# Order of the output products inside a block of a gated-linear-attention, pooling and memory-attention layer on Trainium2

## The chip, the cores and the metric

The kernel runs on one core of one Trainium2 chip. The metric is device time in microseconds (us). The kernel before took 1407.87 us as the median of 3 runs (1406.61 to 1410.97).

## The reference

One decoder layer over `x` of 4096 rows by 1024, with a memory of 256 rows. Three mixers read one input projection, and one output projection adds them back:

```python
h = rmsnorm(x, norm_g)
q_g,k_g,v_g,gk_lr,gate_g,u_p,gate_p,q_m,gate_m = split(h @ w_in)
gk    = log_sigmoid(gk_lr @ w_gk_up + b_gk) / 16          # per-step log decay
o_gla = rmsnorm(gla_chunked(q_g, k_g, v_g, gk)) * silu(gate_g)   # 4 heads, chunks of 64, state carried along
o_pool= (multiscale_pool(u_p) @ pool_w) * pool_scale * silu(gate_p)
o_mem = softmax(q_m k_m^T / 8) v_m * silu(gate_m)         # k_m, v_m from rmsnorm(mem)
y     = rmsnorm(x + concat(o_gla, o_pool, o_mem) @ w_out, final_g)
```

In `gla_chunked` the state of a chunk is the decayed state of the chunk before plus `k_end^T v`; a head's output is its masked scores times `v` plus `q` times the state.

## The kernel before

The sequence is cut into 16 blocks (steps 0 to 15) of 256 rows, each with four chunks of 64. All large products are made of f16 high and low parts, three matmuls for each product. The engines each have their own instruction list and meet at semaphores; the order on each engine is the order in which its code is written. No scheduler changes it. Steps 0 to 3 multiply whole weight blocks (`whole`); steps 4 to 15 use a seven-product form (`phase`, `product`), for which ACT and POOL also make sums and differences of the normalised input.

A step `i` on TensorE (PE) is, in order:

- the low-rank product (L758), the first queries and keys product, then the decay logits (L777), which wait for ACT's copy `lrs` of the low-rank result. That copy (L1183) waits in ACT's queue, and also for `mix_g`, the end of the head products of step `i - 1` on VectorE (DVE), because `lrs` lies in the memory of `osq[1]`;
- all other input products, then the values (`values`, L662 on `wv`);
- transposes, scores and memory scores, and between and behind them the output projection of block `i - 1`, cut into four quarters of 24 matmuls of 128x512 (`quarter(n)`, `out_proj`, L662 on `ring`). Quarters 0 and 2 write PSUM bank 0, quarters 1 and 3 bank 1. Each quarter's result is added on DVE to the residual (`add_rows`, L1633, called `rows(n)`), and a quarter that uses a bank again waits for that addition;
- `states(0)`, `states(1)` (L900): the four chunk products from which DVE builds the carried state, `state(0)` to `state(3)` (L1884, two instructions each);
- `head_out(0, 5)`, `head_out(1, 4)` (L909, L915): the heads' products, the first behind `s_ok` of `state(2)`, the second behind that of `state(3)`;
- the product with the memory's values (L970), which waits for the DMA transposes (`d_turn`) of the softmax weights; it signals `pe_pv`;
- `head_ms(0)`, `head_ms(1)` (L923): sums of squares of the heads, which wait for ACT's squares (L1421).

On DVE the order at that place is `p_low(2)`, `p_low(3)` (L1868, the low parts of the softmax weights, behind ACT's L1377), `rows(1)`, `state(2)`, `state(3)`, `norm_rows`, `rows(2)`, the pool's and the memory's gated products, `rows(3)`, and the two heads (`head`, L1893 and L1895). On ACT, behind the squares of the heads, stand two copies of the input's sums (`x_mixed`, L1067) that wait for `pe_pv`, the Ln and Exp of the heads' norms (L1433, L1436), two more `x_mixed` copies, of which the last waits for a POOL subtraction (L2062) at the end of a chain that the first copy starts, and then `lrs` (L1183). The `x_mixed` copies exist only when the next step uses `phase`, that is ahead of steps 4 to 15.

The SP queue loads the weights of the next step into `ring` slots when quarter 2 and quarter 3 have finished (`pe_out`), and issues the four transposes as the softmax weights are made.

Of the kernel before, what the change touches and what calls it, by code (L numbers as in the profile page):

```python
# [107 lines left out]
def hybrid_block(nc, xt, x, memt, w_qk, w_v, w_qm, w_g, w_p, w_ut, w_gk_up, vecs, pool_w, counts, w_mem, w_out,  # L108
# [3 lines left out]
    with ctx:  # L112
# [488 lines left out]
        def _(pe):  # L601
# [63 lines left out]
            def whole(i, g, row, b):  # L665

                for j in range(2):
                    ap = bank[b][:, j * TB:(j + 1) * TB]
                    for k in range(KT):
                        c, q = 2 * row + k // 4, 2 * (k // 4)  # L670
                        if j == 0 and k % 4 == 0:
                            if i == 0:
                                pe.wait_ge(lo_c, LATER[g] + c + 1)
                            if i >= 2 and g in (GG, PM):
                                pe.wait_ge(d_slot[WHOLE_SLOT[g][c]], 16 * loads("whole", i, WHOLE_SLOT[g][c]))
                        for n, (p, r) in enumerate(((0, 0), (0, 1), (1, 0))):
                            mm = nc.tensor.matmul(ap, whole_parts[g][c][:, p, k % 4, j * P:(j + 1) * P],  # L677
                                                  xs[:, 0, r, q:q + 2, (k % 4) * P:(k % 4 + 1) * P],
                                                  start=k == 0 and n == 0, stop=k == KT - 1 and n == 2)
                mm.then_inc(pe_f[g], 1 + row)  # L680
# [37 lines left out]
            def out_proj(j, n, arrived=None):  # L718

                t, h = n // 2, n % 2  # L720
                if n == 0:
                    pe.wait_ge(m_hi, j + 1)
                    pe.wait_ge(m_lo, j + 1)
                if n >= 2:
                    pe.wait_ge(y_add, 4 * j + n + 3)
                if arrived is not None and t == 0:
                    for s in WO_SLOT[h]:
                        pe.wait_ge(d_slot[s], 16 * loads("out", arrived, s))
                split(bank[h][:, :], KT, lambda k, p, r: (mhl[:, p, k, t * P:(t + 1) * P],
                                                          wo[h][k // 2][:, r, k % 2, :])).then_inc(pe_out, 1)  # L730
# [12 lines left out]
            def step(i, first, second, last):  # L743
# [161 lines left out]
                def head_out(p, b):  # L905

                    for t in range(NT):
                        for h in range(2):
                            nc.tensor.matmul(bank[b][:, h * TB + t * P:h * TB + (t + 1) * P],  # L909
                                             v[:, t, (2 * p + h) * DV:(2 * p + h + 1) * DV],  # L910
                                             sT[:, t, 2 * p + h, :], start=t == 0 and h == 0, stop=False,
                                             skip_group_check=True)
                    o3 = bank[b][:, :].rearrange("p (h t) -> p h t", h=2)
                    for c in range(NC):
                        mm = nc.tensor.matmul(o3[:, :, c * CHUNK:(c + 1) * CHUNK], S[:, c, p, :],  # L915
                                              qb[:, p, :, c * CHUNK:(c + 1) * CHUNK], start=False,
                                              stop=c == NC - 1, skip_group_check=True)
                    mm.then_inc(pe_o, 1)

                def head_ms(p):  # L920

                    pe.wait_ge(o_sq, 2 * i + p + 1)
                    nc.tensor.matmul(bank[6 + p][:, :], ones[:, :], osq[p], start=True,  # L923
                                     stop=True).then_inc(pe_msq, 1)

                def quarter(n):
                    if not first:
                        out_proj(i - 1, n, i)
# [17 lines left out]
                if first:  # L946
                    pe.wait_ge(cp[GG], 4)
                    whole(i, PM, 0, 0)
                quarter(2)
                if first:  # L950
                    pe.wait_ge(ad[GG], 4)
                    whole(i, PM, 1, 1)
# [3 lines left out]
                head_out(0, 5)  # L956
                pe.wait_ge(s_ok, 4 * i + 4)
                head_out(1, 4)
                if not last:
                    quarter(3)  # L960
                for turned in d_turn:
                    pe.wait_ge(turned, 32 * (i + 1))
                pe.wait_ge(p_exp, 4 * i + 3)
# [10 lines left out]
                if last:  # L974

                    head_ms(0)
                    head_ms(1)
                    quarter(3)
                else:
                    head_ms(0)  # L980
                    head_ms(1)

# [14 lines left out]
            for i in range(NB):  # L997
                step(i, i == 0, i == 1, i == NB - 1)
# [1194 lines left out]
```

## Time and profile before

| | |
|---|---|
| median of 3 runs | 1407.87 us |
| the profiled execution, device time | 1410.5 us |
| its span | 1408.6 us |
| PE busy | 1360.8 us, 97% |
| DVE busy | 806.3 us, 57% |
| ACT busy | 750.3 us, 53% |
| POOL busy | 372.6 us, 26% |
| mean granted PE clock | 0.998 |

The profile is of one execution. Its device time is 1.9 us above its span. L numbers are lines of the kernel. A row of a timeline merges neighbouring instructions of one kind: its start, the time it covers, how many there are, and in brackets the idle time of the engine just before it and what ended it. The end of a matmul row is modelled and reaches some 0.15 us past the start of the next row when they follow without a wait, so the distance between starts is the better measure. A granted clock of 1.00 is 2.4 GHz, 0.50 is 1.2 GHz.

### The profile page before, as it was taken

Reading aid. Unit: us, or ns where it says so; the run is one execution under the profiler, and the core shown is the slowest. Engines: PE = TensorE matmul, PEld = TensorE weight load, DVE = VectorE, ACT = ScalarE, POOL = GpSimd, SP = SyncE. Lnnn points to the kernel's source line nnn. Section 1 sums busy time; section 2 is a strip of 40 time slices with the busy share of each in tenths; the row PEclk is TensorE's granted clock in tenths of the full one; section 3 lists DMA queues with packets and bytes.
Section 4 is the critical chain, followed back from the end, with each engine's and each line's share of the span. In section 5 each row is a group of like instructions: output and inputs, shape, how many; then the busy total and the mean of one; then the engine's idle time right before and its main releaser. Section 6 shows DMA issues by size and latency. Waiting matters only on the chain.

```text
span 1408.6 us, 35233 instructions
## 1 busy us (share of the span) xinstructions
PE 1360.8 (97%) x14716; PEld 1013.9 (72%) x14716; DVE 806.3 (57%) x1524; ACT 750.3 (53%) x1380; POOL 372.6 (26%) x313
## 2 busy tenths in 40 slices
PE   4999999999999999999999999999999999999997
PEld 3688658577695967859586685958769596775953
DVE  4886558575555655555555554564555465455454
ACT  5887546555545464454645545464554556445353
POOL 2111155136322242232223322232232224223100
PEclk9999999999999999999999999999999999999999
DMA  9466755663573747456373654637367363755631
GB/s 388 143 192 197 257 180 181 221 226 152 180 265 88 265 118 254 181 180 219 102 294 118 218 220 139 251 90 273 147 193 257 104 254 108 255 181 180 236 96 45
DMA packets 143622, 269.31 MB, mean 191 GB/s; under 512 B 75136, under 2 KB 88704, under 8 KB 140416
## 3 DMA queue, kind: packets, MB, share of 16 engines
q1 hardware_dynamic: 142768, 266.20, 55.0%
q8 instruction: 116, 1.90, 0.5%
q10 hardware_dynamic: 720, 1.06, 0.2%
q14 instruction: 18, 0.15, 0.0%
HBM read 220.03 MB, written 30.41 MB: 178 GB/s over the span
## 4 chain that ended last, share of the span: by engine, by line
PE 81%; issue 7%; POOL 5%; ACT 3%; DVE 2%; DMA 1%; ACTq 0%; SPq 0%; POOLq 0%; DVEq 0%
PE bank L662 29%; PE bank L698 29%; PE bank L677 10%; POOL arena L2039 2%; PE bank L889 2%; PE bank L915 2%; PE bank L909 2%; PE bank L992 1%; POOL arena L2062 1%; PE bank L777 1%; PE bank L900 1%; PE bank L873 1%; DMA out_parts<-fg 1%; PE bank L606 1%; ACT wres L1034 1%
## 5 line engine op out<-in xcount | busy, mean ns | idle before, releaser
L662 PE MATMUL bank<-ring,arena 128*128 128x512 f16 x1440 | 318.3, 379 | 0.0
L662 PEld LDWEIGHTS bank<-ring,arena 128*128 128x128 f16 x1440 | 139.7, 98 | 162.9 <-issue 3.1
L698 PE MATMUL bank<-arena,ring 128*128 128x128 f16 x4032 | 237.1, 219 | 0.0
L698 PE MATMUL bank<-arena,wres 128*128 128x128 f16 x4032 | 237.0, 219 | 0.0
L698 PEld LDWEIGHTS bank<-arena,ring 128*128 128x128 f16 x4032 | 228.4, 98 | 5.2 <-DVE arena L1552 1.8
L698 PEld LDWEIGHTS bank<-arena,wres 128*128 128x128 f16 x4032 | 227.7, 98 | 2.5 <-issue 2.5
L662 PE MATMUL bank<-wv,arena 128*128 128x512 f16 x768 | 170.2, 382 | 0.0
L2024 POOL TENSOR_TENSOR arena<-arena 128x1024 f32<-128x1024 f32 (+2 forms) x42 | 65.4, 1557 | 353.8 <-ACT arena L1040 351.6
L662 PEld LDWEIGHTS bank<-wv,arena 128*128 128x128 f16 x768 | 75.6, 98 | 90.0 <-issue 2.2
L2032 POOL TENSOR_TENSOR arena<-arena 128x1024 f16<-128x1024 f32 x32 | 67.5, 2131 | 200.2 <-ACT arena L1058 200.2
L1633 DVE SCALAR_TENSOR_TENSOR arena<-bank,sca,arena 128x512 f32<-128x512 f32 x60 | 44.9, 748 | 90.8 <-DMA arena<-in_x 90.3
L677 PE MATMUL bank<-arena,wres 128*128 128x256 f16 x768 | 88.3, 277 | 0.0
L1558 DVE SCALAR_TENSOR_TENSOR arena<-bank,sca,arena 128x256 f32<-128x256 f32 x48 | 23.2, 484 | 109.8 <-ACT arena L1146 109.8
L677 PE MATMUL bank<-arena,ring 128*128 128x256 f16 x768 | 85.3, 273 | 0.0
L677 PEld LDWEIGHTS bank<-arena,wres 128*128 128x128 f16 x768 | 76.0, 100 | 11.3 <-issue 0.6
L1067 ACT ACTIVATE arena<-arena 128x512 f16<-128x512 f32 x48 | 28.7, 621 | 102.1 <-PE bank L970 73.1
L1856 DVE TENSOR_REDUCE mx<-bank 128x2 f32<-128x512 f32 x64 | 41.1, 684 | 72.1 <-PE bank L889 72.1
L2039 POOL TENSOR_TENSOR arena<-arena 128x512 f16<-128x512 f32 x48 | 60.4, 1267 | 80.9 <-ACT arena L1067 80.9
L677 PEld LDWEIGHTS bank<-arena,ring 128*128 128x128 f16 x768 | 75.1, 98 | 8.8 <-issue 0.2
L1868 DVE SCALAR_TENSOR_TENSOR arena<-arena,rsum 128x256 f16<-128x256 f32 x128 | 54.9, 481 | 43.3 <-ACT arena L1377 43.3
L1146 ACT ACTIVATE arena<-bank,sca 128x256 f32<-128x256 f32 x48 | 22.5, 468 | 94.5 <-PE bank L698 94.5
L1367 ACT ACTIVATE arena<-bank,nm,sca 128x256 f32<-128x256 f32 x128 | 71.0, 559 | 3.1
(247 smaller groups left out, 2036.5 us busy)
## 6 DMA issues: line engine op xcount, KB each, us to landing
ring<-out_parts SPq DMA_DIRECT2D x120, 512.0 KB, 5.6
ring<-gate_parts SPq DMA_DIRECT2D x92, 512.0 KB, 6.1
ring<-side_parts SPq DMA_DIRECT2D x92, 512.0 KB, 6.7
arena<-in_xt SPq DMA_DIRECT2D x16, 1024.0 KB, 6.2
arena<-in_x SPq DMA_DIRECT2D x32, 512.0 KB, 4.5
out<-arena SPq DMA_DIRECT2D x31, 512.0 KB, 2.8
arena<-in_w_out SPq DMA_DIRECT2D x16, 512.0 KB, 5.6
out_parts<-arena SPq DMA_DIRECT2D x6, 512.0 KB, 6.9
```

Source lines behind the costliest of these rows:

```text
L662: mm = nc.tensor.matmul(ap, lhs, rhs, start=k == 0 and n == 0, stop=(k, n) == last)
L677: mm = nc.tensor.matmul(ap, whole_parts[g][c][:, p, k % 4, j * P:(j + 1) * P], xs[:, 0, r, q:q + 2, (k % 4) * P:(k % 4 + 1) * P], start=k ...
L698: mm = nc.tensor.matmul(ap, w[:, p, k, j * P:(j + 1) * P], x_part(r, b)[:, k, :], start=fresh and j == 0 and k == 0 and n == 0, stop=k == ...
L889: mm = nc.tensor.matmul(bank[b][:, h * NMEM:(h + 1) * NMEM], qst[:, p, h, t * P:(t + 1) * P], kst[:, p, h, r, :], start=r == 0, stop=r == 1)
L1067: nc.scalar.activation(x_part(0, b), sg[(m - 1) % 2], ACT.Copy).then_inc(x_hi, 1)
L1367: a = nc.scalar.activation(pr[n % 2][:, h, :], bank[2 + n % 2][:, h * 256:(h + 1) * 256], ACT.Exp, bias=nm[:, 2 * n + h:2 * n + h + 1], sc ...
L1633: nc.vector.scalar_tensor_tensor(yb[:, c], bank[h][:, :], sc_out, yb[:, c], ALU.mult, ALU.add).then_inc(y_add, 1)
L1856: nc.vector.tensor_reduce(mx[:, 2 * n:2 * n + 2], bank[2 + n % 2][:, :].rearrange("p (h m) -> p h m", h=2), AX.X, ALU.max).then_inc(max_ok, 1)
L1868: a = nc.vector.scalar_tensor_tensor(phl[n % 2][:, 1, h, :], pr[n % 2][:, h, :], rsum[:, 2 * n + h:2 * n + h + 1], phl[n % 2][:, 0, h, :], ...
L2024: nc.gpsimd.tensor_tensor(sq[:, 0:half, :], sq[:, 0:half, :], sq[:, half:2 * half, :], ALU.add).then_inc(sq_add, 1)
L2032: nc.gpsimd.tensor_tensor(ap[1], xb[:, 4 * k:4 * k + 4, :].rearrange("p k (b t) -> p k b t", b=2), ap[0], ALU.subtract).then_inc(x_lo, 1)
L2039: nc.gpsimd.tensor_tensor(x_part(1, b), sg[(m - 3) % 2], x_part(0, b), ALU.subtract).then_inc(x_lo, 1)
```

## The change

In `step` of the PE program `quarter(2)` moves from behind `quarter(1)` to behind `head_out(1, 4)`, and `quarter(3)`, in all steps but the last, from there to behind the product with the memory's values, ahead of `head_ms`. In the last step `quarter(3)` stays behind `head_ms`. No other engine's program is touched; lines behind the change move up by one or two.

```diff
                 if first:
                     pe.wait_ge(cp[GG], 4)
                     whole(i, PM, 0, 0)
-                quarter(2)
                 if first:
                     pe.wait_ge(ad[GG], 4)
                     whole(i, PM, 1, 1)
...
                 head_out(0, 5)
                 pe.wait_ge(s_ok, 4 * i + 4)
                 head_out(1, 4)
-                if not last:
-                    quarter(3)
+                quarter(2)
                 for turned in d_turn:
                     pe.wait_ge(turned, 32 * (i + 1))
...
                     head_ms(1)
                     quarter(3)
                 else:
+                    quarter(3)
                     head_ms(0)
                     head_ms(1)
```

PE, the back half of a step that is neither the first nor the last, before. L662 are quarters (24 matmuls each), L900 the chunk products, L909 and L915 the heads, L970 the memory's values, L923 the sums of squares:

```order
L900 MATMUL bank<-arena 64x128 x16
L662 MATMUL bank<-ring,arena 128x512 x48
L909 MATMUL bank<-arena 128x128 x4
L915 MATMUL bank<-arena 128x2x64 x4
L909 MATMUL bank<-arena 128x128 x4
L915 MATMUL bank<-arena 128x2x64 x4
L662 MATMUL bank<-ring,arena 128x512 x24
L970 MATMUL bank<-arena,vm 64x256 x24
L923 MATMUL bank<-arena,ones 128x512 x2
L758 MATMUL bank<-arena,wlr 32x256 x16
```

The same place in the changed kernel (L968 is L970 of before):

```order
L900 MATMUL bank<-arena 64x128 x16
L662 MATMUL bank<-ring,arena 128x512 x24
L909 MATMUL bank<-arena 128x128 x4
L915 MATMUL bank<-arena 128x2x64 x4
L909 MATMUL bank<-arena 128x128 x4
L915 MATMUL bank<-arena 128x2x64 x4
L662 MATMUL bank<-ring,arena 128x512 x24
L968 MATMUL bank<-arena,vm 64x256 x24
L662 MATMUL bank<-ring,arena 128x512 x24
L923 MATMUL bank<-arena,ones 128x512 x2
L758 MATMUL bank<-arena,wlr 32x256 x16
```

One quarter instead of two stands ahead of the heads, and one quarter now stands between the memory's values and the sums of squares.

DVE at the same time, in the changed kernel, with the semaphores waited for; it is the order of before with line numbers one higher. L1867 are the softmax weights' low parts, L1632 is `rows(1)`, the L1883 that follow are `state(2)` and `state(3)`:

```order
L1867 SCALAR_TENSOR_TENSOR arena<-arena,rsum 128x256 [waits p_hi]
L1867 SCALAR_TENSOR_TENSOR arena<-arena,rsum 128x256
L1632 SCALAR_TENSOR_TENSOR arena<-bank,sca,arena 128x512 [waits pe_out,sc_ok]
L1883 SCALAR_TENSOR_TENSOR arena<-arena,dec,bank 128x128 [waits s_ok,pe_st]
L1883 SCALAR_TENSOR_TENSOR arena<-arena,dec,bank 128x128
L1883 SCALAR_TENSOR_TENSOR arena<-arena,dec,bank 128x128 [waits s_ok,pe_st]
```

Nothing moved on DVE: `rows(1)`, which waits for the end of quarter 1, still stands ahead of the states that the heads' products wait for.

## Rows read from the trace of the kernel before

**Rows 1.** Waits of PE: what waited, for whom, total us, times, longest.
```profile
PE bank L777 <- ACT arena L1183: 14.4, 13, 1.1
```

**Rows 2.** Timeline of PE, a middle block: start, us covered, line, shapes, count.
```profile
772.72 10.53 PE L662 MATMUL bank<-ring,arena 128*128 128x512 f16 x48
783.09 1.05 PE L909 MATMUL bank<-arena 128*128 128x128 f32 x8
...
786.66 5.34 PE L662 MATMUL bank<-ring,arena 128*128 128x512 f16 x24
791.93 1.50 PE L970 MATMUL bank<-arena,vm 128*64 128x256 f16 x24
793.36 1.98 PE L923 MATMUL bank<-arena,ones 128*128 128x512 f32 x4
...
795.83 4.19 PE L698 MATMUL bank<-arena,wres 128*128 128x128 f16 x72
801.15 1.13 PE L777 MATMUL bank<-arena,up 128*128 128x256 f32 x4 [1.13 <-ACT arena L1183]
```

**Rows 3.** Timeline of DVE, the same block; the third row from a narrower window.
```profile
777.88 1.68 DVE L1868 SCALAR_TENSOR_TENSOR arena<-arena,rsum 128x256 f16<-128x256 f32 x4 [0.63 <-ACT arena L1377]
779.47 0.74 DVE L1633 SCALAR_TENSOR_TENSOR arena<-bank,sca,arena 128x512 f32<-128x512 f32 x1
780.14 0.60 DVE L1884 SCALAR_TENSOR_TENSOR arena<-arena,dec,bank 128x128 f32<-128x128 f32 x2
...
789.74 0.75 DVE L1633 SCALAR_TENSOR_TENSOR arena<-bank,sca,arena 128x512 f32<-128x512 f32 x1 [6.46 <-DMA arena<-in_x]
```

**Rows 4.** The same two engines in step 1: PE, then DVE.
```profile
182.16 10.53 PE L662 MATMUL bank<-ring,arena 128*128 128x512 f16 x48
...
189.50 1.31 DVE L1884 SCALAR_TENSOR_TENSOR arena<-arena,dec,bank 128x128 f32<-128x128 f32 x4
```

**Rows 5.** Timeline of ACT, the middle block again.
```profile
793.55 1.15 ACT L1067 ACTIVATE arena<-arena 128x512 f16<-128x512 f32 x2 [6.10 <-PE bank L970]
...
800.11 0.63 ACT L1067 ACTIVATE arena<-arena 128x512 f16<-128x512 f32 x1 [2.41 <-POOL arena L2062]
800.65 0.46 ACT L1183 ACTIVATE arena<-bank,sca 128x256 f32<-128x256 f32 x1
```

**Rows 6.** Last step: PE's sums of squares, DVE's last head product.
```profile
1371.85 1.98 PE L923 MATMUL bank<-arena,ones 128*128 128x512 f32 x4
...
1376.51 0.69 DVE L1895 TENSOR_TENSOR arena<-bank,arena 128x512 f32<-128x512 f32 x1
```

**Rows 7.** DVE and PE at the start of step 2.
```profile
208.01 2.12 DVE L1893 TENSOR_TENSOR arena<-arena 128x512 f32<-128x512 f32 x1
...
211.47 1.13 PE L777 MATMUL bank<-arena,up 128*128 128x256 f32 x4 [0.79 <-ACT arena L1183]
```

**Rows 8.** SP's transposes in the middle block, and issues: count, KB, us to landing.
```profile
770.84 10.61 SPq L458 DMA_TRANSPOSE arena<-arena  x4
...
arena<-arena SPq DMA_TRANSPOSE x4, 3.1
...
ring<-gate_parts SPq DMA_DIRECT2D x92, 512.0 KB, 6.1
```

**Rows 9.** PE idles of about 2.5 us, and the matmuls behind the first.
```profile
160.38 0.67 PE L606 MATMUL bank<-arena,ones 128*128 128x256 f32 x2 [2.47 <-DVE arena L1574]
160.89 12.21 PE L662 MATMUL bank<-wv,arena 128*128 128x512 f16 x48
...
1381.64 20.88 PE L992 MATMUL bank<-ring,arena 128*128 128x512 f16 x96 [2.45 <-DVE arena L1974]
```

**Rows 10.** Stretches: length, busy (count) of PE, PEld, DVE, ACT, POOL, PEclk, DMA share, GB/s.
```profile
162.00:163.00 1.00, 1.00 (x4) 0.40 (x3) 0.00 (x0) 0.97 (x3) 0.00 (x0) 0.50 1.04 426
...
1379.00:1382.00 3.00, 0.55 (x5) 0.33 (x4) 2.33 (x8) 2.01 (x4) 0.00 (x0) 1.00 0.00 0
```

## The prediction

> **What bounds the kernel now.** I read the busy shares first: PE is busy 97% of the span, so only two things can move the time, a wait of PE that goes or one that comes. The list of PE's waits, read next, shows one that recurs: the logits wait for ACT's low-rank copy 13 times, 14.4 us in all [rows 1]; 12 of these stand in steps 4 to 15, 1.06 us once and 1.13 or 1.14 otherwise, the 13th, 0.79 us, in step 2 [rows 7]. The others are at the start, ahead of the values of step 1, and in the tail. So I read the timeline of one middle block for PE [rows 2], then that of DVE and ACT in the same microseconds [rows 3, 5]: who would be late if PE came 5 us earlier, and who early.
>
> **Durations.** Two quarters take 783.09 - 772.72 = 10.37 us from start to start, one 5.18 us. The two heads take 786.66 - 783.09 = 3.57 us and the memory's values 793.36 - 791.93 = 1.43 us [rows 2]. No matmul is added or removed: the change costs or gives only waits.
>
> **Part one: quarter 2 leaves its place ahead of the heads.** In the middle block quarter 1 ends at 772.72 + 5.18 = 777.90, and the heads then stand next on PE. They wait for state(2). DVE makes the low parts of the softmax weights until 779.56, because it waits there for ACT, then rows(1) from 779.47, then state(2), two instructions that end at 780.14 + 0.60 = 780.74 [rows 3]. With 0.04 us of signalling (as from the end of L1183, 800.65 + 0.46, to the logits at 801.15 [rows 2, 5]) the heads start at 780.78: PE stands for 780.78 - 777.90 = 2.88 us. Before, quarter 2 covered this with 2.3 us to spare. Nothing on DVE or ACT ahead of this point depends on the moved work, since the chain that feeds it hangs on the memory scores and on quarters 0 and 1, so the wait is not made up. state(3) ends 0.7 us later while the first head (1.8 us) runs, so the second does not wait. Step 1 has the same distance: the states start 189.50 - 182.16 = 7.34 us behind quarter 1, against 780.14 - 772.72 = 7.42 us here [rows 2 to 4]. The wait comes in steps 1 to 15, the last included: 15 x 2.88 = +43.2 us. Queued behind the waiting head on PE is everything else, so the full amount counts.
>
> **Part two: the memory's values come earlier against the end of the step.** The wait before the logits is ended by a long chain: the values' end lets ACT start the copies of the input's sums (793.55), POOL subtracts, ACT copies the last sum at 800.11 when POOL has made it, and only then, 800.65, the low-rank copy [rows 5]. With quarter 3 behind the values this chain starts 5.18 us earlier against all that follows. POOL's last result was there at about 800.08, 8.15 us behind the values' start (791.93). The sums of squares now start 1.43 + 5.18 = 6.61 us behind it, so POOL is ready 1.5 us behind the start of the sums of squares. The ACT copies no longer hold the low-rank copy.
>
> What is late next is the head chain: sums of squares, Ln and Exp, two products per head on DVE, then the low-rank copy. The last step shows it without POOL beside it: from 1371.85 to 1376.51 + 0.69 = 1377.20, 5.35 us [rows 6]. Add 0.06 to start, 0.46 for the copy and 0.04: the logits may start 5.91 us behind the sums of squares. PE reaches them after 795.83 - 793.36 + 4.03 = 6.50 us (the 72 small matmuls cover 4.19 us, less the 0.16 by which a row overlaps the next, 10.53 against 10.37 for two quarters) [rows 2]. It has 0.59 us to spare and the wait is gone. Start to start the wait is worth 801.15 - (795.83 + 4.03) = 1.29 us, since the bracket counts from a modelled end. For 11 such and one 0.07 us shorter: 12 x 1.29 - 0.07 = 15.4 us less. The bounds of this term are 0 (the wait stays) and -15.4.
>
> The row that speaks against it is in step 2: beside POOL's work a head product that takes 0.68 us in the last step took 2.12 us, and PE waited [rows 7]. In the changed steps only POOL's last two subtractions fall beside the second head. If the product beside them stretches as in step 2 the chain is 1.4 us longer, 7.3 against 6.5 us, and 0.8 us of the wait stays. That is rival two. The Trainium skill, GPSIMD Engine Reference, section Specifications, says that GpSimd shares its SBUF interfaces with VectorE and contends with its instructions that have two SBUF inputs, as these products do; the trace agrees (2.12 us against 0.68), and by that rule alone each step would keep some wait.
>
> **The other edges, at nothing.** The values' product waits for the transposes: issued until 770.84 + 10.61 = 781.45, 3.1 us to landing [rows 8], so down by 784.6; it now starts at 780.78 + 3.57 + 5.18 = 789.5, 4.9 us later. rows(2) waited for the residual's DMA until 789.74 [rows 3]; quarter 2 now ends at the same time, and nothing waits for rows(2) before the next step's first products, 8 us on. rows(3) ends 0.9 us behind quarter 3; the sums of squares (1.9 us) cover it. Gate weights load behind quarters 2 and 3: issued from 789.5, 2 us of issuing and 6.1 us to land [rows 8], about 798, for a use at about 804; if that cover were gone it would cost what the DMA is late by, some us a step. The second lot has as much. In step 2 POOL is at work as before, so its 0.79 us stays.
>
> **The clock.** The new idles are 2.9 us long. The trace has two of nearly that length: behind the one of 2.47 us the granted clock fell from 2.4 to 1.2 GHz (0.50) for some 3.5 us, and 48 matmuls took 12.21 us against 10.53, 1.7 us more; behind the one of 2.45 us it stayed at 1.00 [rows 2, 9, 10]. So 15 idles may cost from 0 to 15 x 1.7 = 25 us. The trace doesn't tell what decides. I take 2 of 15, 3.4 us: the low side, because both idles were single and a stretch at the low level also moves everything behind it, so that the same thing need not happen again in the next step.
>
> **The sum.** 43.2 - 15.4 + 3.4 = +31.2 us. The profiled execution would be 1410.5 + 31.2 = 1441.7 us; it was itself 2.6 us above the median of the runs, so against the median 1407.87 + 31.2 = 1439.1 us; I predict 1439, slower by 2.2%.
>
> **The rivals.**
> - One, the forecast: the wait for the state comes, that for the copy goes, the clock falls seldom: 1439 us, 1435.7 to 1446 with none to six falls. Chance 0.66.
> - Two: the head chain, or POOL beside it, keeps the wait before the logits, so the gain is between 0 and 1.29 x 12. At no gain: 1407.87 + 43.2 + 3.4 = 1454.5 us. For it: step 2. Against it: 0.59 us to spare and POOL's chain over before the first head. Chance 0.13.
> - Three: the clock falls behind most of the new idles: 1407.87 + 27.8 + 14 to 25 = 1450 to 1461 us (8 to 15 falls). For it one of two rows, against it the other. Chance 0.13.
> - Four, the other side: the heads' wait doesn't come, because state(2) is ready when quarter 1 ends. Then only the gain is left, 1407.87 - 15.4 = 1392.5 us. It decides at a wait of 15.4 / 15 = 1.03 us: below that the change wins. It needs DVE to reach state(2) 1.9 us sooner than 780.14, but DVE stands there behind ACT's copies of softmax weights [rows 3], whose order doesn't change. Chance 0.04. The small rest, 0.04, is a smaller wait that cancels or nearly cancels, or one that I don't see.
>
> A change of up to 0.3% (4.2 us) is what a measurement of this kernel can't tell from none. Faster has 0.04, same 0.03, slower 0.93. The range goes from 1431 (the wait 0.3 us shorter per step and no fall of the clock) to 1456, which takes in rival two and the lower part of three.
>
> **What would show it.** A PE wait at L909 for DVE's state, 15 times, about 2.7 us each in brackets; no wait at L777 but those of steps 0 to 3; ACT's low-rank copy released by DVE's last head product instead of POOL; DVE's rows(1) still 779.47 - 772.72 = 6.75 us behind the start of quarter 1; the granted clock below 1.00 in few stretches behind the idles. A wait at the memory's values or at the gate products, or no wait at L909, would make the prediction wrong.

## The result, and the profile after

The changed kernel took 1449.33 us (median of 4 runs, 1448.18 to 1449.94) against 1407.61 us before (4 runs): ratio 1.0291, 95% interval 1.0272 to 1.0310. It is 41.7 us slower. The forecast was 31.2 us slower, 1439, with a range from 1431 to 1456. The profiled execution took 1448.18 us, its span is 1446.3 us, the mean granted PE clock 0.989 against 0.998.

The list of PE's waits in the changed kernel (what waited, for whom, total us, times, longest), the answer to [rows 1]:

```profile
PE bank L909 <- DVE arena L1883: 42.0, 15, 2.8
...
PE bank L777 <- ACT arena L1182: 0.5, 1, 0.5
```

The wait that was there before steps 4 to 15 is gone. One with three times its sum stands at the heads' products, in all of steps 1 to 15.

The timeline of PE in a step in which the clock stayed up (start, us covered, line, shapes, count, idle before), the front part of what [rows 2] shows of before:

```profile
700.64 5.35 PE L662 MATMUL bank<-ring,arena 128*128 128x512 f16 x24
708.81 1.13 PE L909 MATMUL bank<-arena 128*128 128x128 f32 x8 [2.82 <-DVE arena L1883]
709.78 1.06 PE L915 MATMUL bank<-arena 128*128 128x128 f32 x8
```

Quarter 1 starts at 700.64, so it ends at 705.82, and the heads start at 708.81, 2.99 us later; 2.88 was forecast. The heads of the step ahead started at 623.70: the step is 85.11 us long, against 83.49 before, +1.62 us. The prediction's two terms make 2.88 - 1.29 = +1.59. The difference is right; the experiments show below that each term by itself is about 0.16 us larger.

DVE ahead of the heads of another step, the answer to [rows 3]:

```profile
878.90 1.68 DVE L1867 SCALAR_TENSOR_TENSOR arena<-arena,rsum 128x256 f16<-128x256 f32 x4 [0.63 <-ACT arena L1376]
880.49 0.75 DVE L1632 SCALAR_TENSOR_TENSOR arena<-bank,sca,arena 128x512 f32<-128x512 f32 x1
881.15 1.31 DVE L1883 SCALAR_TENSOR_TENSOR arena<-arena,dec,bank 128x128 f32<-128x128 f32 x4
```

DVE is where the sum put it: softmax weights behind ACT, rows(1), then the states. The same step on PE:

```profile
873.73 5.35 PE L662 MATMUL bank<-ring,arena 128*128 128x512 f16 x24
881.90 2.04 PE L909 MATMUL bank<-arena 128*128 128x128 f32 x8 [2.82 <-DVE arena L1883]
883.74 1.80 PE L915 MATMUL bank<-arena 128*128 128x128 f32 x8
885.37 1.06 PE L909 MATMUL bank<-arena 128*128 128x128 f32 x8
```

`rows(1)` starts 880.49 - 873.73 = 6.76 us behind the start of quarter 1; 6.75 was forecast. The wait is the same 2.82 us, but the first head's products take about twice as long as in the step shown above (2.04 against 1.13 us); the second head's take 1.06 us again. That is the clock. A table of stretches of 4 us, each from the start of the heads' products, says how often this happens (start and end, length, busy times and counts of PE, PEld, DVE, ACT, POOL, then the granted clock, the DMA share and GB/s), the answer to [rows 10]:

```profile
708.81:712.81 4.00, 4.00 (x34) 3.83 (x35) 1.85 (x3) 1.77 (x6) 0.02 (x1) 1.00 0.67 168
793.93:797.93 4.00, 4.00 (x19) 4.00 (x20) 1.84 (x3) 1.23 (x5) 0.00 (x0) 0.50 0.65 165
881.90:885.90 4.00, 4.00 (x21) 4.00 (x22) 1.85 (x3) 1.35 (x5) 0.00 (x0) 0.58 0.65 165
968.63:972.63 4.00, 4.00 (x34) 3.83 (x35) 1.84 (x3) 1.77 (x6) 0.03 (x1) 1.00 0.65 166
```

Of the 15 such stretches 7 are below 1.00 (0.50 to 0.66); these four rows are steps 7 to 10. At 0.50 TensorE runs at 1.2 GHz. From 793.93 it stays there for 6 us; the next heads start 87.97 us later instead of 85.11, so this fall cost 2.9 us. The one at 881.90 cost 86.73 - 85.11 = 1.6 us.

ACT at the end of a changed step, the answer to [rows 5]:

```profile
815.89 1.13 ACT L1066 ACTIVATE arena<-arena 128x512 f16<-128x512 f32 x2
817.62 0.47 ACT L1182 ACTIVATE arena<-bank,sca 128x256 f32<-128x256 f32 x1 [0.60 <-DVE arena L1894]
```

The last copies of the input's sums no longer wait for POOL, and the low-rank copy is released by DVE's last head product. PE in the same step:

```profile
812.34 1.88 PE L923 MATMUL bank<-arena,ones 128*128 128x512 f32 x4
814.14 0.62 PE L758 MATMUL bank<-arena,wlr 128*32 128x256 f16 x16
814.70 4.19 PE L698 MATMUL bank<-arena,wres 128*128 128x128 f16 x72
818.73 1.08 PE L777 MATMUL bank<-arena,up 128*128 128x256 f32 x4
```

The copy ends at 818.09, 5.75 us behind the start of the sums of squares (5.87 forecast), and PE comes at 818.73 without a wait.

### The profile page after: what moved, and what is told of

Same layout as the page of the kernel before. It is cut to its first block, busy times and chain, and to the rows that moved or that the text cites. A ratio compares the mean times of both kernels' runs of the same rounds, so it can differ in the third digit from the quotient of the medians.

```text
span 1446.3 us, 35233 instructions
## 1 busy us (share of the span) xinstructions
PE 1370.8 (95%) x14716; PEld 1024.2 (71%) x14716; DVE 789.1 (55%) x1524; ACT 753.9 (52%) x1380; POOL 365.8 (25%) x313
## 3 DMA queue, kind: packets, MB, share of 16 engines
q10 hardware_dynamic: 720, 1.06, 0.2%
## 4 chain that ended last, share of the span: by engine, by line
PE 77%; ACT 9%; DVE 8%; issue 3%; DMA 1%; POOL 1%; SPq 0%; ACTq 0%; DVEq 0%; POOLq 0%
PE bank L698 31%; PE bank L662 22%; PE bank L677 9%; ACT arena L1366 4%; DVE arena L1867 3%; PE bank L909 3%; PE bank L915 2%; ACT arena L1376 2%; PE bank L923 2%; PE bank L968 1%; PE bank L991 1%; DVE arena L1632 1%; DVE mx L1855 1%; PE bank L777 1%; ACT nm L1356 1%
## 5 line engine op out<-in xcount | busy, mean ns | idle before, releaser
L662 PE MATMUL bank<-ring,arena 128*128 128x512 f16 x1440 | 320.9, 379 | 0.0
L662 PEld LDWEIGHTS bank<-ring,arena 128*128 128x128 f16 x1440 | 138.6, 98 | 162.2 <-issue 5.9
L662 PE MATMUL bank<-wv,arena 128*128 128x512 f16 x768 | 168.5, 379 | 0.0
L662 PEld LDWEIGHTS bank<-wv,arena 128*128 128x128 f16 x768 | 75.1, 98 | 88.8
L1632 DVE SCALAR_TENSOR_TENSOR arena<-bank,sca,arena 128x512 f32<-128x512 f32 x60 | 45.0, 749 | 168.2 <-PE bank L662 159.7
L2038 POOL TENSOR_TENSOR arena<-arena 128x512 f16<-128x512 f32 x48 | 56.8, 1194 | 122.3 <-ACT arena L1066 122.3
L909 PE MATMUL bank<-arena 128*128 128x128 f32 x256 | 43.0, 322 | 42.0 <-DVE arena L1883 42.0
L1867 DVE SCALAR_TENSOR_TENSOR arena<-arena,rsum 128x256 f16<-128x256 f32 x128 | 54.9, 481 | 43.4 <-ACT arena L1376 43.4
L909 PEld LDWEIGHTS bank<-arena 128*128 128x128 f32 x256 | 38.6, 230 | 49.0 <-issue 49.0
```

The lines of the kernel that those rows point to most:

```text
L662: mm = nc.tensor.matmul(ap, lhs, rhs, start=k == 0 and n == 0, stop=(k, n) == last)
L1632: nc.vector.scalar_tensor_tensor(yb[:, c], bank[h][:, :], sc_out, yb[:, c], ALU.mult, ALU.add).then_inc(y_add, 1)
L1867: a = nc.vector.scalar_tensor_tensor(phl[n % 2][:, 1, h, :], pr[n % 2][:, h, :], rsum[:, 2 * n + h:2 * n + h + 1], phl[n % 2][:, 0, h, :], ...
L2038: nc.gpsimd.tensor_tensor(x_part(1, b), sg[(m - 3) % 2], x_part(0, b), ALU.subtract).then_inc(x_lo, 1)
```

## The experiments

In every experiment the four DMA transposes of a step are replaced by plain DMA copies of the same bytes, so the softmax weights reach the product with the memory's values untransposed, and the memory's part of the output differs.:

```diff
-                sp.dma_start_transpose(out=pt[:, p, :, t * P:(t + 1) * P],
-                                       in_=phl[n % 2].rearrange("p r h m -> p (r h m)")).then_inc(d_turn[n % 2], 16)
+                sp.dma_start(pt[:, p, :, t * P:(t + 1) * P],
+                             phl[n % 2].rearrange("p r h (m t) -> p (r h m) t", t=P)).then_inc(d_turn[n % 2], 16)
```

The number of DMAs and the semaphores stay as they are. A copy lands 3.0 us after its issue, a transpose 3.1 us (medians).

**The two controls.** The kernel before with this edit alone:

> A control: the kernel before with the four DMA transposes of each step replaced by plain DMA copies of the same bytes into the same places, so the softmax weights reach the product with the memory's values untransposed. The order of all engines is that of before, and the copies wait and signal as the transposes did. The copies should land within about the 3.1 us of the transposes, which had 5 us to spare, so every theory expects the time of before, 1407 to 1409, with the same wait before the logits.

1409.66 us (8 runs) beside 1409.84 for the kernel before: ratio 0.9996 (0.9983 to 1.0010). Its list of PE's waits has the same 14.4 us, 13 times, before the logits.

> A control: the changed kernel with the four DMA transposes of each step replaced by plain DMA copies of the same bytes, as in the control of the kernel before. Expected as the changed kernel: 1448 to 1450, the wait at the heads 2.8 us in 15 steps, none before the logits in steps 4 to 15, and a few stretches of lower clock behind the idles. Were it the transposes that the changed order had made late, this one would differ from 1449.

1449.26 us (3 runs), ratio 1.0291 (1.0269 to 1.0312), the same as the changed kernel's own. The wait at the heads is 41.8 us in 15 steps. The four runs of the changed kernel and the three of this one lie between 1448.18 and 1451.32 us. So the copies stand in for the transposes, and the transposes are no part of the loss. The clock fell behind 8 of the 15 idles. This kernel and the next three had the same runs of the kernel before beside them, 1408.53 us.

**Quarter 3 moved, quarter 2 left in its place.**

```diff
                 head_out(1, 4)
-                if not last:
-                    quarter(3)
                 for turned in d_turn:
...
                 else:
+                    quarter(3)
                     head_ms(0)
```

> The second part of the change alone (quarter 2 stays ahead of the heads, quarter 3 goes behind the memory's values), on the control with plain copies. Theory A (the loss is PE's wait for the state, and the values coming earlier removes the wait before the logits): no wait at the heads, none at the logits in steps 4 to 15, 15.4 us below the control, about 1393. Rival B (the logits' wait is kept by the heads' own chain): about 1408. Rival C (quarter 3 so late disturbs something else, the weight loads or the bank): above 1411.

1393.48 us (3 runs, 1392.41 to 1393.89), ratio 0.9890 (0.9870 to 0.9909): 15.05 us faster than before, 15.4 were expected. PE in the middle of it:

```profile
691.49 1.05 PE L909 MATMUL bank<-arena 128*128 128x128 f32 x8
692.38 1.06 PE L915 MATMUL bank<-arena 128*128 128x128 f32 x8
693.28 1.06 PE L909 MATMUL bank<-arena 128*128 128x128 f32 x8
694.17 1.06 PE L915 MATMUL bank<-arena 128*128 128x128 f32 x8
695.16 1.50 PE L968 MATMUL bank<-arena,vm 128*64 128x256 f16 x24
696.59 5.35 PE L662 MATMUL bank<-ring,arena 128*128 128x512 f16 x24
701.78 1.88 PE L923 MATMUL bank<-arena,ones 128*128 128x512 f32 x4
...
708.17 1.08 PE L777 MATMUL bank<-arena,up 128*128 128x256 f32 x4
```

No row has a bracket: no wait at the heads, none at the memory's values, which now follow them directly, and none at the logits (L777). The one wait left before the logits is that of step 2:

```profile
PE bank L777 <- ACT arena L1182: 0.9, 1, 0.9
```

Rivals B and C are out. This half of the change is a gain.

A step of this kernel is 82.05 us long from heads to heads, against 83.49 before: 1.44 us, and not the 1.29 of the sum. In 12 steps that is about 17 us. That the medians show only 15.05 has one likely reason, which is not shown for each run: the clock also falls behind idles that all these kernels have, and not in every execution. The last products (L991, L992 before) stand behind one of them. In the profile of before they took 20.88 us [rows 9]; in this kernel's profile, behind an idle of the same length, they took 1.7 us more:

```profile
1362.04 22.57 PE L991 MATMUL bank<-ring,arena 128*128 128x512 f16 x96 [2.45 <-DVE arena L1973]
```

**Quarter 2 moved, quarter 3 behind it, both ahead of the memory's values.**

```diff
                 head_out(1, 4)
                 quarter(2)
+                if not last:
+                    quarter(3)
                 for turned in d_turn:
...
                 else:
-                    quarter(3)
                     head_ms(0)
```

> The first part alone (quarter 2 behind the heads, quarter 3 behind quarter 2, both ahead of the memory's values), on the control with plain copies. Theory A: the full wait for the state (15 x 3.0 us) and the full wait before the logits, with some falls of the clock: 13 to 17 us above the changed kernel, about 1462 to 1466. Rival: the idle at the heads lets the chain before the logits catch up, so that the wait there goes without part two: about 1449.

1469.99 us (3 runs), ratio 1.0433 (1.0412 to 1.0453). It is 20.7 us above the changed control, where 13 to 17 had been expected. Both waits are there in full:

```profile
PE bank L909 <- DVE arena L1884: 41.9, 15, 2.8
PE bank L777 <- ACT arena L1183: 14.0, 13, 1.1
```

The rival is refuted: the idle at the heads does not help the chain before the logits, since that chain starts behind it. The loss is 5.3 us more than the 15.4 of the logits' wait, and the expectation missed by 3.7 us or more. The trace gives two parts. A step in which the clock stays up takes 86.55 us against 85.10 in the changed control, 1.45 us more, which makes about 17.4 us in 12 steps, 2 more than 15.4. And the clock fell behind 10 of 15 idles against 8; a step with such a fall takes 88.18 us, 1.6 us more, which makes another 3.3 us.

**The changed kernel with the states first on DVE.**

```diff
                 state(0)
                 state(1)
+                state(2)
+                state(3)
                 p_norm(2)
                 p_norm(3)
                 p_low(2)
                 p_low(3)
                 rows(1)
-                state(2)
-                state(3)
```

> The changed kernel, on the control with plain copies, with one more edit on VectorE: state(2) and state(3) stand directly behind state(0) and state(1), ahead of the softmax weights and of rows(1). Theory A: the states are ready at about 777.2 in the block where PE wants them at 777.9, the wait at the heads goes, the clock stays up, about 1393. Rival (the heads' wait is for something other than the order of VectorE, for instance the chunk products): still near 1449. If the softmax weights, now about 1 us later, made PE wait at the memory's values, that would show as 1 us a step, about 1408.

1393.76 us (3 runs), ratio 0.9890 (0.9871 to 0.9909): the whole loss and the gain on top. PE:

```profile
764.26 5.35 PE L662 MATMUL bank<-ring,arena 128*128 128x512 f16 x24
769.45 1.05 PE L909 MATMUL bank<-arena 128*128 128x128 f32 x8
```

The heads start 5.19 us behind quarter 1, with no wait. What they waited for was the place of two states in DVE's list, not the length of any work: all the same instructions are still executed. The softmax weights, which now come later, cost nothing that shows: a step takes 82.05 us, as with quarter 3 moved alone.

The next four had other runs of the kernel before beside them, 1408.82 us (11 runs).

**The same order of DVE in the kernel before.**

> The kernel before, on the control with plain copies, with state(2) and state(3) directly behind state(0) and state(1) on VectorE, both quarters where they were. Theory A: PE did not wait there, so nothing changes, 1408 to 1410, and the wait before the logits stays 1.1 us in steps 4 to 15. Rival (part of the gain of the kernel with the states first came from VectorE's order itself): below 1404.

1409.59 us (9 runs), ratio 1.0007 (0.9996 to 1.0017), the wait before the logits 14.4 us as before. The order of DVE is worth nothing while quarter 2 covers it.

**The wait filled.** Ahead of the wait for the states:

```diff
+                if not first:
+                    pe.wait_ge(y_add, 4 * i + 1)
+                    for n in range(12):
+                        nc.tensor.matmul(bank[0][:, :], mhl[:, 0, n % 8, P:2 * P], wo[0][n % 4][:, 0, n % 2, :],
+                                         start=True, stop=True)
                 pe.wait_ge(sT_ok, 2 * i + 1)
```

> The changed kernel, on the control with plain copies, with 12 spare 128x512 matmuls in steps 1 to 15 ahead of the heads' products, in the time in which PE waits for the state; they write bank 0, which quarter 2 then overwrites, so nothing of the result depends on them. Theory D (the falls of the clock behind the idles are about 12 of the 41 us): what matters waits as long as before, but PE is not idle, the clock stays at 1.00, and the time is 1408.5 + 15 x 3.0 - 15.4 = about 1438. Rival (what the falls cost is hidden elsewhere, or the waits are longer than read): 1449 as the changed kernel, or above it by what the spare matmuls overrun.

1436.98 us (3 runs, 1434.35 to 1437.46), ratio 1.0193 (1.0173 to 1.0213). PE does more work than in the changed control and is 12.3 us faster. The heads still start when the states are there:

```profile
792.11 1.13 PE L909 MATMUL bank<-arena 128*128 128x128 f32 x8 [0.22 <-DVE arena L1888]
793.08 1.06 PE L915 MATMUL bank<-arena 128*128 128x128 f32 x8
```

The mean clock of its profile is 0.998, and it is 1.00 behind all 15 places. Two terms come from this: against quarter 3 moved alone the waits for the states are 1436.98 - 1393.48 = 43.5 us, and the clock's falls are 1449.26 - 1436.98 = 12.3 us. Both are differences of medians of three runs, and the three runs of the filled kernel spread over 3.1 us. Step by step the traces say the same more closely. A filled step takes 85.09 us against 82.05 with quarter 3 moved alone: 3.04 us for the wait, 45.6 us in 15 steps. In the changed control a step in which the clock stays up has the same length as a filled one, and the seven steps 1, 2, 3, 8, 9, 13 and 14, in which it falls, are 1.4 to 3.0 us longer, 13.8 us together. The eighth fall is in the last step.

**A shorter wait.** `state(2)` and `state(3)` ahead of `rows(1)`, behind the softmax weights:

```diff
                 p_low(3)
-                rows(1)
                 state(2)
                 state(3)
+                rows(1)
```

> The changed kernel, on the control with plain copies, with state(2) and state(3) one place earlier on VectorE, ahead of rows(1) but behind the softmax weights. Theory A: the wait at the heads is shorter by rows(1), 0.67 us, so 2.15 us instead of 2.82 in brackets, 15 x 0.67 = 10 us less, and if the clock falls seldom behind such an idle another 5 to 12 us less: 1427 to 1439. Rival (the wait is for the end of quarter 1, through rows(1)): the whole wait goes, 1393.

1440.17 us (3 runs), ratio 1.0217 (1.0197 to 1.0237), 1.2 us above what was expected. The wait shrank as forecast:

```profile
PE bank L909 <- DVE arena L1883: 32.0, 15, 2.2
```

The rival (that rows(1) and the end of quarter 1 are the cause) is out: three quarters of the wait are still there, and what DVE does in them is the softmax weights and then the states themselves. But the other hope failed. Without falls this kernel should take 1393.5 + 32.0 + 15 x 0.16 for the overlap of rows = 1427.9 us; it took 12.3 us more, and the clock was below 1.00 behind 8 of its 15 idles. Two of the stretches, with and without a fall:

```profile
876.47:880.47 4.00, 4.00 (x34) 3.83 (x35) 2.22 (x4) 2.29 (x6) 0.02 (x1) 1.00 0.55 125
960.92:964.92 4.00, 4.00 (x21) 4.00 (x22) 2.22 (x4) 2.07 (x5) 0.00 (x0) 0.57 0.56 125
```

A step without a fall takes 84.44 us, one with a fall 86.07: 1.6 us each. So in this kernel the idles of 2.2 us cost as much clock as those of 2.8 us did in the control.

**Both remedies together.** Quarter 3 moved, quarter 2 in its place, the states first.

> Quarter 3 behind the memory's values, quarter 2 where it was, and the states first on VectorE, on the control with plain copies. Both edits remove or forestall waits that are already gone with quarter 3 moved alone, so theory A gives the same time as that, 1392 to 1394. A faster one would mean that a wait is left that the profile doesn't show.

1392.43 us as the median of 1391.02, 1392.43 and one run of 4184.7 us that nothing here explains; the ratio without that run is 0.9877 (0.9853 to 0.9901), which overlaps that of quarter 3 moved alone. As expected, there is no third wait to remove. The versions without the wait at the heads, 1392.4 to 1393.8 us, are the only ones that beat the kernel before, by 1.1 to 1.2%; they were run with the plain copies only.

## Why the prediction was right, and where it was mis-sized

- **Direction and mechanism: right.** PE waits at the heads for state(2) in 15 steps, released by DVE, and the wait before the logits goes in steps 4 to 15. Each was isolated: moving only quarter 3 gives the gain, moving only quarter 2 gives the loss, and reordering two calls on DVE takes the loss away.
- **The wait for the state: right, a little small.** 43.2 us in the sum, 43.5 by the medians with the wait filled, 45.6 by the steps of the traces (3.04 us each instead of 2.88). The heads start 2.99 us behind quarter 1, and the first matmuls behind such a wait are slower: 0.97 us from start to start (708.81 to 709.78) against 0.89 without a wait (691.49 to 692.38).
- **The logits: right, a little small.** 15.4 us in the sum, 15.05 by the medians, about 17 by the steps of the traces (1.44 us each instead of 1.29). That the medians hit both terms so closely is in part luck. Per step the two errors are of one size and cancel, so that the net +1.59 us of the sum stands beside +1.62.
- **The head chain: right.** It kept its forecast place behind the sums of squares (5.75 against 5.87 us), and rival two is out. The premise of that rival was half right: only the first of a head's two products on DVE reads two SBUF operands (`arena<-arena`). It took 1.34 and 0.92 us in the middle block of before, where POOL was at work beside it, and 0.69 and 0.68 us in the changed step shown (from 814.85), where POOL's subtraction that feeds ACT had ended 1.7 us before. The second, which reads a PSUM bank, took 0.69 us in all steps of both kernels.
- **The edges at nothing: right.** With quarter 3 moved alone PE has no wait at the memory's values or at the gate products. The changed kernel's own list has none there either. Step 2 kept a wait (0.5 us in the changed kernel, 0.79 before).
- **The clock: the term that was mis-sized.** The sum had 2 falls of 15 and 3.4 us. The profile shows 7, in the control 8, and the filled wait puts them at 12.3 us. The number 2 stood on an argument and on no row; the falls beyond it are 8.9 of the 10.2 us by which the forecast was short. The argument for the low side ("the same thing need not happen again in the next step") failed: the clock did fall in neighbouring steps (2 and 3, 8 and 9, 13 to 15) and was up in steps 4 to 7 and 10 to 12. The two rows of before, one fall in two idles, were the better guide: 7.5 falls of 1.7 us are 12.7 us.
- **What is left**, 1.3 us, is within the spread of the runs.
- **The rivals.** The measured 1449.33 lies between rival one (up to 1446, none to six falls) and rival three (from 1450, 8 to 15 falls), as 7 falls should. Rival four needed a wait under 1.03 us and the wait was 2.9.

What decides behind which idle the clock falls was not settled. The pattern of steps is the same in the profiles of the changed kernel and its control from step 2 on, and all four runs of the changed kernel have the same mean clock, 0.989, so for these idles it is hardly chance from run to run. In step 1 the clock fell in the control alone, and behind the idle of 2.45 us ahead of the last products it stayed up in the profile of before and fell in that of its control.

## What to carry to other kernels

A quarter of work that stands ahead of a wait is a cover: before moving it, read on the other engine when the waited-for result is ready, and compare with where the moved work would have ended. Two moves in one change can have opposite signs, and then each is worth trying alone: here one half gained 1.1% and the other lost four times that. If the cover has to go, look first at the order on the engine that is waited for; two short calls behind work that the waiting engine did not need yet were the whole loss.

## What the runs showed of the hardware

In this kernel an idle of TensorE cost more than its length. The granted clock dropped from 2.4 to 1.2 GHz behind 8 of 15 idles of 2.2 us, and behind 7, 8 and 10 of 15 idles of 2.8 us in three kernels. A fall made its step 1.6 us longer as a rule and 2.9 us in the longest cases; with 8 falls that is about 12.3 us, or 0.8 us per idle. Twelve spare matmuls in the idle kept the clock up and made the kernel 12.3 us faster while doing more work. Besides, the matmuls right behind an idle took 0.97 us for eight instead of 0.89 with the clock up.
